# Result rows of the experts written row by row through GpSimd's queue, instead of whole blocks through ScalarE's

## The reference

```
N_GROUPS = 4; EXPERTS_PER_GROUP = 8; TOP_K = 2; D_EXPERT = 512
x = x + hierarchical_moe(rms_norm_2(x, norm_ffn[l]), ...)   # for each token:
    # two chosen experts e of its group, with gates g:  sum of g * down_e(silu(gate_e(h)) * up_e(h))
return rms_norm_2(x, norm_final)
```

## Time and profile before

| | |
|---|---|
| median of 3 runs | 2068.24 us (2066.67 to 2074.23) |
| span of the profiled execution | 2067.1 us; no other time of that execution is given |
| PE busy | 1994.4 us, 96% of the span |
| DVE, ACT, POOL busy | 45%, 28%, 18% |
| all 32 experts | from 1463.8 to 2016.1 us, 552 us |
| granted PE clock | 0.99 to 1.00 but in the last stage |

### The profile page before, as it was taken

How to read it: one execution, slowest core, us unless ns; L and a number is a source line. 1 busy time by engine, 2 the same in 40 slices (tenths; PEclk the granted TensorE clock), 3 DMA queues, 4 the chain that set the end, 5 groups by cost and what they waited for, 6 DMA issues and landing times.

```text
span 2067.1 us, 37980 instructions
## 1 busy us (share of the span) xinstructions
PE 1994.4 (96%) x15588; PEld 1136.0 (55%) x15588; DVE 932.4 (45%) x1543; ACT 583.1 (28%) x1076; POOL 376.2 (18%) x317
## 2 busy tenths in 40 slices
PE   8999999999899999999999999998999999999997
PEld 6476564765434445454446454565666666666563
DVE  3434553455676753586666674344511111111115
ACT  4123231433575220243123422242111111111113
POOL 0304333325252003004000233000100000000003
PEclk9999999999999999999999999999999999999999
DMA  9221220212525023600030412012899999999987
GB/s 396 84 82 36 81 95 28 94 31 87 173 102 173 31 103 64 166 1 1 0 122 11 143 42 64 1 41 91 346 398 402 406 407 414 416 405 412 404 355 269
DMA packets 104554, 360.51 MB, mean 174 GB/s; under 512 B 20536, under 2 KB 59856, under 8 KB 90128
## 3 DMA queue, kind: packets, MB, share of 16 engines
q1 hardware_dynamic: 58016, 280.37, 34.7%
q0 software_dynamic: 16368, 55.85, 8.0%
q10 hardware_dynamic: 30080, 23.09, 3.4%
HBM read 319.16 MB, written 45.49 MB: 176 GB/s over the span
## 4 chain that ended last, share of the span: by engine, by line
PE 72%; DMA 13%; DVE 8%; ACT 4%; issue 2%; ACTq 1%; POOL 0%; DVEq 0%; POOLq 0%; SPq 0%; PEldq 0%
PE bank L741 18%; DMA y_of_slot<-HT 13%; PE bank L734 12%; PE bank L951 9%; PE bank L1622 8%; PE bank L1638 4%; ACT work L1742 3%; PE bank L977 2%; PE bank L1037 2%; DVE O L2291 1%; DVE work L2291 1%; PE bank L809 1%; PE bank L1375 1%; PE bank L1152 1%; PE bank L849 1%
## 5 line engine op out<-in xcount | busy, mean ns | idle before, releaser
L1742 ACT ACTIVATE HT<-bank 64x256 f32<-64x256 f32 (+2 forms) x215 | 91.9, 432 | 452.5 <-PE bank L1622 197.0
L1742 ACT ACTIVATE work<-bank 128x512 f32<-128x512 f32 (+5 forms) x246 | 123.2, 520 | 327.4 <-PE bank L741 96.0
L1742 ACT ACTIVATE work<-work 128x1024 f32<-128x1024 f32 (+5 forms) x200 | 158.9, 806 | 170.4 <-DVEq L149 114.7
L734 PE MATMUL bank<-slots,HT 128*128 128x512 f32 (+2 forms) x576 | 184.1, 475 | 2.0 <-ACT HT L1742 1.5
L1622 PE MATMUL bank<-slots,HT 128*32 128x256 f32 x3136 | 172.4, 379 | 2.5 <-DVE HT L3148 1.6
L1622 PE MATMUL bank<-work,HT 128*32 128x256 f32 x3072 | 168.9, 379 | 0.4 <-issue 0.4
L3268 POOL TENSOR_TENSOR work<-work 128x1024 f32<-128x1024 f32 (+1 forms) x64 | 112.0, 1750 | 241.8 <-DVEq L149 160.6
L3154 DVE TENSOR_TENSOR HT<-HT,bank 64x256 f32<-64x256 f32 x97 | 41.1, 423 | 242.8 <-ACT HT L1742 242.4
L1622 PEld LDWEIGHTS bank<-slots,HT 128*32 128x32 f32 x3136 | 103.1, 110 | 68.8 <-issue 3.2
L734 PEld LDWEIGHTS bank<-slots,HT 128*128 128x128 f32 x576 | 98.3, 190 | 76.6 <-issue 71.2
L1622 PEld LDWEIGHTS bank<-work,HT 128*32 128x32 f32 x3072 | 102.4, 110 | 64.2 <-issue 1.0
(11 more groups left out here) (352 smaller groups left out, 3091.1 us busy)
## 6 DMA issues: line engine op xcount, KB each, us to landing
slots<-in_w_e_gate_dram SPq DMA_DIRECT2D x17, 2048.0 KB, 13.5
slots<-in_w_e_up_dram SPq DMA_DIRECT2D x17, 2048.0 KB
slots<-in_w_e_down_dram SPq DMA_DIRECT2D x17, 2048.0 KB, 17.4
work<-in_w_e_gate_dram SPq DMA_DIRECT2D x16, 2048.0 KB, 13.2
work<-in_w_e_up_dram SPq DMA_DIRECT2D x16, 2048.0 KB
work<-in_w_e_down_dram SPq DMA_DIRECT2D x16, 2048.0 KB
slots<-in_w_in_dram SPq DMA_DIRECT2D x8, 2048.0 KB, 8.7
slots<-in_w_ada_dram SPq DMA_DIRECT2D x6, 2048.0 KB, 15.3
```

The source lines that it names most:

```text
L734: ins = pe.matmul(bank, lhsT, rhs, start=(n == 0), stop=(n == len(pairs) - 1))
L1742: return act.activation(o, i, f, bias=bias, scale=scale, **more)
```

## The change

Of the result array all 32 x 96 rows and the 58 spare blocks are cleared by POOL's early transfer, 154 blocks of 32 rows in place of 58. ACT's stores of the experts are gone. In their place POOL, in its loop, waits after the gather for e + 2 until the result of e is in `YO[x]`, copies three columns of indices, and issues three indirect transfers, one for each group of slots, with 128 indices each (row r and quarter q of the group). DVE works the indices out once: for a slot that is not filled the index gets 2^20 added, is out of bounds, and nothing is written. `y_stored[x]` now rises by 48 for each expert. The first two experts don't wait for it. ACT's loop has its first pass written out. The stores of the spare blocks stay with ACT.

```
-            ("iota", P), ("slot_of_row", CAP), ("token", NT)):
+            ("iota", P), ("slot_of_row", CAP), ("token", NT),
+            ("slot_of_piece", TGS), ("piece_of_y", EXPERTS * TGS)):
...
-        y_experts = y_dram[0:EXPERTS * CAP].rearrange("(b p) d -> b p d", p=CAP)
+        y_pieces = y_dram.rearrange("r (q c) -> (r q) c", c=QW)
...
 ACT, for each expert
-                    act.wait_ge(y_stored[x], it * 64 + 64)
+                if not first:
+                    act.wait_ge(y_stored[x], it * 48)
                     act.wait_ge(down_full, it * 4 + 2 * x + 1)
                     func(YO[x][:, 0:HALF], DOWN_BANKS[0], ACT.Copy).then_inc(y0_out, 1)
-                    act.wait_ge(y0_out, it * 2 + x + 2)
-                    act.wait_ge(y1_out, it * 2 + x + 2)
-                    store_block(it * 2 + x, YO[x], y_stored[x])
...
 DVE, once
+            ts(ASSIGNED, SPN, (CAP + 1 - TG) / TG - BELOW, float(TG), ALU.add, ALU.mult)
...
+                tt(cut(PIECES, EXPERTS), bcast(const("slot_of_piece").unsqueeze(1), each), bcast(ASSIGNED.unsqueeze(2), each),
+                   ALU.is_ge)
+                stt(piece_list[:, :], PIECES, BEYOND_Y, const("piece_of_y"), ALU.mult, ALU.add)
...
 POOL, once
-            pool.dma_start(y_spares.rearrange("b p d -> p b d"),
-                           zeros[0:TG, :].unsqueeze(1).to_broadcast([TG, SPARE, D])).then_inc(spare_cleared, 16)
+            pool.dma_start(y_dram.rearrange("(b p) d -> p b d", p=TG),
+                           zeros[0:TG, :].unsqueeze(1).to_broadcast([TG, SPARE + EXPERTS * TGS, D])).then_inc(spare_cleared, 16)
...
 POOL, for each expert
                     gather_block(x, XG[x], rows_gathered[x])
+                    pool.wait_ge(y0_out, it * 2 + x + 2)
+                    pool.wait_ge(y1_out, it * 2 + x + 2)
+                    pool.tensor_copy(pieces[x][:, :], piece_list[:, bass.ds((it * 2 + x) * TGS, TGS)]).then_inc(pieces_ready, 1)
+                    pool.wait_ge(pieces_ready, it * 2 + x + 1)
+                    pool.sem_inc(pool_passed, 1)
+                    for g in range(TGS):
+                        pool.indirect_dma_start(y_pieces, bass.IndirectOffsetOnAxis(ap=pieces[x][:, g:g + 1], axis=0),
+                                                YO[x][:, g * QW:(g + 1) * QW], None, bounds_check=EXPERTS * CAP * 4 - 1,
+                                                oob_is_err=False).then_inc(y_stored[x], 16)
```

More of the change, by code:

```diff
@@ L634, in program @@
         spare_map = ctx.enter_context(nc.sbuf_tensor("spare_map", [P, SPARE + 1], I32))
+        piece_list = ctx.enter_context(nc.sbuf_tensor("piece_list", [P, EXPERTS * TGS], U32))
+        pieces = [ctx.enter_context(nc.sbuf_tensor(f"pieces{x}", [P, TGS], U32)) for x in range(2)]
+        pieces_ready = sem("pieces_ready")
         index = [ctx.enter_context(nc.sbuf_tensor(f"index{x}", [P, 1], U32)) for x in range(3)]
@@ L648, in program @@
         EMPTY = temp(BLOCKS)
+        ASSIGNED, PIECES = temp(EXPERTS), temp(EXPERTS * TGS)
         SPN, INC, KE, BEHIND, CN = temp(EXPERTS), temp(EXPERTS), temp(EXPERTS), temp(EXPERTS), temp(SPARE + 1)
@@ L2216, in hidden_home, with expert @@
                 func(HIDT[:, a, :, :], cut(HIDDEN_BANKS[a], 4)[:, 0:2, :], ACT.Copy).then_inc(back, 1)
[L2218 to L2223, removed]
-                for x in range(2):
[L2225 to L2230, removed]
-                    act.wait_ge(y_stored[x], it * 64 + 64)
-                    act.wait_ge(down_full, it * 4 + 2 * x + 1)
-                    func(YO[x][:, 0:HALF], DOWN_BANKS[0], ACT.Copy).then_inc(y0_out, 1)
-                    act.wait_ge(y0_out, it * 2 + x + 2)
-                    act.wait_ge(y1_out, it * 2 + x + 2)
-                    store_block(it * 2 + x, YO[x], y_stored[x])
-            act.wait_ge(y_stored[0], 64 * (EXPERTS // 2 + 1))
+            def expert(it, x, first=False):
+                for g in range(TGS):
+                    act.wait_ge(group_full, it * 6 + 3 * x + g + 1)
+                    silu_of(g, silu_ready)
+                for a in range(2):
+                    act.wait_ge(hidden_turned, it * 4 + 2 * x + a + 1)
+                    hidden_home(a, hidden_back)
+                if not first:
+                    act.wait_ge(y_stored[x], it * 48)
+                act.wait_ge(down_full, it * 4 + 2 * x + 1)
+                func(YO[x][:, 0:HALF], DOWN_BANKS[0], ACT.Copy).then_inc(y0_out, 1)
+            for x in range(2):
+                expert(0, x, True)
+            with act.Fori(1, EXPERTS // 2) as it:
+                for x in range(2):
+                    expert(it, x)
+            act.wait_ge(y_stored[0], 24 * EXPERTS)
             spare = spare_count(act)
@@ L3162, in token_lists @@
                 tell("pool")
-                for x in range(2):
-                    dve.sem_inc(y_stored[x], 64)
                 dve.sem_inc(y0_out, 1)
@@ L3185, in gates_and_slots, with expert @@
                 copy(slot_id[:, :], SLOT)
+                each = [P, EXPERTS, TGS]
+                tt(cut(PIECES, EXPERTS), bcast(const("slot_of_piece").unsqueeze(1), each), bcast(ASSIGNED.unsqueeze(2), each),
+                   ALU.is_ge)
+                stt(piece_list[:, :], PIECES, BEYOND_Y, const("piece_of_y"), ALU.mult, ALU.add)
                 dve.sem_inc(routed, 1)
-            def expert(it, x, first=False):
+            def expert(it, x, first=False, second=False):
                 for g in range(TGS):
@@ L3201, in expert @@
                     gates_and_slots()
-                dve.wait_ge(y_stored[x], it * 64 + 64)
+                if not (first or second):
+                    dve.wait_ge(y_stored[x], it * 48)
                 dve.wait_ge(down_full, it * 4 + 2 * x + 2)
@@ L3209, in _ @@
             block_ready(tokens_ready)
-            for x in range(2):
-                expert(0, x, first=(x == 0))
+            expert(0, 0, first=True)
+            expert(0, 1, second=True)
             with dve.Fori(1, EXPERTS // 2) as it:
```

8 lines of the change are left out of this document (6 added, 2 removed).

## The result

The changed kernel takes 2105.99 us (median of 4 runs, 2103.47 to 2108.84), the one before 2067.45 us beside it (2065.70 to 2074.23): a ratio of 1.0178, 95% interval 1.0162 to 1.0194. It is slower by 1.8%. The prediction, 2070.0 us with a range of 2064 to 2090, missed it. The profiled execution has a span of 2103.1 us, 36.0 more than the 2067.1 of before.

What follows compares the result with a forecast made beforehand. PE was taken to bound the kernel, with the DMA engines full too. Against the 2067.1 us span, -2.4 + 0.2 + 3 + 0.6 + 0.5 = +1.9 gave 2069.0; with the median 1.1 above the span, 2070, range 2064 to 2090.

Steps and rivals of the forecast that it cites:

- The step that failed: POOL in the loop: its copy, wait and three issues add 4.9 us to each 17.06, delaying nobody except by their order.
- The queue's turns: DMA engines in the loop: queues take equal turns of packets, q0 having 34 against q1's 27, 0.632 us a turn.
- Late by 1.4 us in the first round: Gather behind the stores: lands at S + 29.2, where PE needs it at S + 27.8, S being an expert's start.
- +3: Early experts: PE's total wait for the late gather, the middle of 0 to 6.3 us, in us.
- Rivals 2 and 3: Before each expert's block turn: q0's extra packets pass slowly, up to 2123, chance 0.25; or never catch up, 2200, chance 0.05.
- Rival 1: Loop: the queue doesn't matter or the start costs nothing, so no late gather; 2066 us, chance 0.22.
- ACT's stores gone: -2.4: Loop: without ACT's four store issues for each expert, PE's two waits of 0.51 and 1.87 us go; -2.4 us.
- DVE +0.2: Ahead of the first expert: one more DVE step of 0.22 us delays `block_ready` and PE behind it; +0.2 us.
- The clearing hidden: Before the first expert: the larger clearing takes 102 us, 811 to 913, before POOL's next work at 953.83; no cost.
- The end: +0.5: After the last expert: POOL's last three stores delay the gather after the spare block's; +0.5 us (0 to 2).
- The late gather: At the end: gather for the block after the spare one lands near 2026, moving PE's next work by 0 to 2 us.
- slower by over 0.5%: Whole kernel: the outcome held by the rivals of dear or absent catching up in the queue; chance 0.30.

Runs made afterwards that it cites:

- e7_spaced: Changed kernel, all three transfers, the second and third each held until PE has multiplied a group of the next expert; 2067.16 us, ratio 0.9994.
- e6_two: Changed kernel with only the transfers of the first two groups of slots issued for each expert, the third left out; 2066.83 us, ratio 0.9993.
- e11_ninety: Changed kernel with 96 indices in each of the three transfers in place of 128; 2071.79 us, ratio 1.0020.
- e4_clear: Kernel before with only the early clearing of all result rows added, ACT's stores kept; 2069.12 us, ratio 1.0005.
- e3_gather: Changed kernel with the three transfers going the other way, reading from the result array into the same buffer; 2106.25 us, ratio 1.0182.
- e5_later: Changed kernel with the three transfers issued half an expert later, behind the next gather, beside the down products; 2104.58 us, ratio 1.0177.
- e9_light: Changed kernel with weight loads cut from 16 to 2 KB a partition from the third expert on; 2066.32 us, ratio 0.9993.
- e12_pair: Changed kernel, all three transfers, only the third held until PE has multiplied the next expert's group 1; 2067.92 us, ratio 0.9996.

## Why the prediction was wrong

**The step that failed** is the one on POOL: "Nobody waits for POOL's time but for its order, priced above." POOL's three issues were costed as 0.98 us each on an engine with time to spare, and the only wait looked for was one in the graph of semaphores. What the runs showed in its place: three transfers of 128 indices in a row, beside DMA engines full of weight loads, take 1.16 us from PE in each expert, with no semaphore between them. From the first expert's start to the spare block's PE takes 585.5 us, where e7_spaced takes 550.0: 35.6 us for the 31 experts that pay it. Against the kernel before (553.2) it is 32.3, since that one lost 3.2 us to waits of its own. e6_two and e7_spaced take the hold-up away whole. In the loop of before GpSimd's transfers with indices come one at a time, and several in a row only at the end, where no weights are loaded. That row even spoke for my costing: 16 transfers of 128 indices, 0.30 us apart, and PE works on beside them at its pace, with the DMA engines kept busy by q0 itself. By windows, the kernel before:

```profile
2036.00:2040.00 4.00, 4.00 (x10) 1.73 (x10) 1.50 (x2) 0.00 (x0) 3.26 (x3) 1.00 1.00 349
```

So no row shows the effect, and that was itself the sign: a row of three beside weight loads was a form that the trace didn't hold, and I bounded it by its own length alone.

**The queue's turns** were the step I took to be the risk, and it was mis-sized. I counted 27 packets for each engine for the three transfers, since the gather makes 7. It was 9 (48 packets for each transfer; if 16 of them are ends, as I take it, each of the other 32 holds four pieces of 1 KB), so q0 had 15.8 turns in a period of 27, never fell behind, and the gather landed in 6.0 us, before 10.4. (With the DMA engines full, as in e11_ninety, it is 10.0.) "Late by 1.4 us in the first round" and "+3" measured 0. The rule that equal turns are taken between queues, on which the earlier trace rows rested, was not refuted; there were only fewer packets to take turns for. Rivals 2 and 3 lose their premise with it; no run has put 34 packets of q0 against 27 of q1, so what that would cost stays untested. Rival 1 was right about the queue, and its 2066 us is near the 2067.16 that e7_spaced measured.

**ACT's stores gone: -2.4** was right in kind. In e7_spaced the loop is busy 410.00 of 410 us, and neither of the waits of the earlier trace rows is left; against the 409.49 of the earlier trace rows. Of the whole time it makes 1.2 us less (3.3 less to 0.8 more, by the ratio's interval), which holds the -2.2 of rival 1 and can't be told from nothing. From the first expert to the spare block it is 3.2 us less than before, 1.0 of it ahead of 1536 us, where the prediction hadn't looked. And the stores may not have all the credit. Ahead of the silu that PE waited 1.87 us for, ACT not only stores but loads a table, once in two experts, in the timeline of before:

```profile
1955.60 1.28 ACT L1742 ACT_TABLE_LOAD   x1 [2.28 <-issue]
```

That load is gone from the loop in the changed kernel and in every run made from it, and e4_clear, made from the one before, still has it. The prediction has no term for it, and no run parts it from the stores.

**DVE +0.2**: `block_ready` ends 0.03 us later and the first expert starts 0.03 later (1463.87 for 1463.84). Right, and smaller.

**The clearing hidden** was right. The timeline of POOL after, the clearing and POOL's next work:

```profile
808.83 1.84 POOL L3451 DMA_DIRECT2D y_of_slot<-masks  x1 [0.30 <-POOL masks L3450]
953.70 1.27 POOL L3279 TENSOR_TENSOR work<-slots 128x512 f32<-128x512 f32 x1 [143.03 <-DVEq L2310]
```

```profile
y_of_slot<-masks POOLq DMA_DIRECT2D x1, 19712.0 KB, 105.7
```

It landed in 105.7 us for the 102 reckoned, and POOL's next work starts where it did. e4_clear confirms it alone.

**The end: +0.5** measured +3.6, and not by the gather. Beside the last three transfers the hold-up comes once more, in the timeline of after:

```profile
2049.40 3.66 PE L1629 MATMUL bank<-slots,HT 128*32 128x256 f32 x64 [0.96 <-DVE HT L3215]
2050.23 1.02 POOL L3556 DMA_INDIRECT y_of_slot<-HT,pieces  x1 [0.88 <-POOL pieces L3552]
...
2054.74 0.38 ACT L1749 ACTIVATE HT<-bank 64x256 f32<-64x256 f32 x1 [7.31 <-remote]
...
2055.63 0.47 PE L1635 MATMUL bank<-cst,HT 128*128 128x128 f32 x2 [2.57 <-DVE HT L3162]
...
2056.67 3.21 PE L1645 MATMUL bank<-slots,HT 128*32 128x256 f32 x32 [0.56 <-ACT HT L1749]
```

PE waits 2.57 us where it waited 0.95 before and in e7_spaced, and the 32 down products take 3.21 us for 1.93: 2.9 of the 3.6 us. The second part is the clock, by the windows of these products in the kernel after, then in e7_spaced:

```profile
2056.67:2059.80 3.13, 3.13 (x32) 1.51 (x32) 0.00 (x0) 0.00 (x0) 0.00 (x0) 0.58 0.02 5
```

```profile
2019.60:2021.60 2.00, 1.93 (x32) 1.13 (x32) 0.00 (x0) 0.00 (x0) 0.84 (x1) 1.00 0.05 8
```

The granted clock is 0.58 in place of 1.00, behind a PE that had done little since 2053: the hold-up itself took 1.6 us, and the lower clock 1.3 more. The late gather that I had priced is seen where the hold-up is gone, in e7_spaced:

```profile
2023.18 0.88 PE L1620 MATMUL bank<-cst,HT 96*128 96x96 f32 x8 [1.62 <-DMA HT<-xn,index]
```

It waits 1.62 us, within the 0 to 2 given, and costs nothing in the end: from the spare block's start it is 50.1 us to the end, there and before.

This last hold-up comes when q1 has no more packets, and when q0 has already moved the first transfer's 48, here in 2051 to 2052 us and in 2052 to 2052.5 of the kernel after:

```profile
q0 software_dynamic: 17, 0.07, 19.7%
...
q0 software_dynamic: 31, 0.06, 35.4%
```

The last three of e7_spaced (2014.72, 2016.05, 2017.34) stand just as near each other, with the same 48 packets gone before the third, and hold nobody up. By ACT's first silu there, 5.3 us after the start of PE's products in place of 3.7, only the kernel after, e3_gather and e5_later have it, the three that have it in the loop; e9_light and e12_pair, with three in a row at the same place, don't. So what went before counts too, and the runs don't say how.

**The chances.** I gave slower by over 0.5% 0.30, all of it through the queue's turns, and 0.12 above 2100, where the result lies. That the sign and the size had any chance at all was luck: it stood on the queue's turns, and the mechanism that came was not among the rivals.

## What to carry to other kernels

A move of work to an idle engine is not costed by that engine's spare time: if it issues several transfers with indices in a row beside heavy weight loads, look at PE's weight loads, and at other engines' waits that have no releaser, in the microseconds after them. Here two of 128 indices in a row were free and three were not; a small copy with its wait before the third, which put it back by 0.8 us, was the whole cure. When a block of matmuls gets longer with no wait ahead of it, its pace is the thing to read, and leaving out one issue at a time finds the cause faster than reasoning about queues.

## What the runs showed that I had not expected

- The hold-up is a step: three transfers with 368 indices in a row are free and with 384 cost 1.16 us of PE for each row of transfers, whichever direction the data go.
- It needs DMA engines full of weights in the loop: at a share of 0.25 the same three transfers are free. Yet it comes once more at the end with a share near 0.1, in just the kernels that had it in the loop, and 16 such transfers in a row behind the experts leave PE's pace alone, before or after.
- A wait of PE can cost more than its length: behind the 2.57 us at the end the granted clock was 0.58, and 32 products took 3.21 us in place of 1.93.
- A transfer of 128 pieces of 1 KB with indices makes 48 packets in the queue, while the kernel's gather of 96 rows of 4 KB makes 112. Four plain transfers of 96 such pieces from GpSimd make 48 each too, where ScalarE's made 112 (28 for each engine and expert by the earlier trace rows, so 28 x 16 / 4).
- Skipped rows take packets: at most 2048 of 3072 rows are filled, so at least a third of the pieces are empty, and e7_spaced has 6152 / 24 = 256 packets for an expert all the same, 112 and three times 48.
